# Window values projected straight into token-major form, instead of transposed after the projection

## The reference

```python
h = rmsnorm(x, norm_mix[l])
aq, ak, av, bq, bk, bv, cin = split_last(h @ w_in[l], IN_SIZES)      # widths 256,128,128,512,512,512,1024
o_win = window_gqa(aq, ak, av, ...)      # 4 query heads, 2 key/value heads of 64, keys within +-128 tokens
o_diff = diff_attention(bq, bk, bv, ...) # 4 heads, two softmax maps each, all 1024 keys
o_rwkv = rwkv7_bidir(cin, ...)           # centred short convolution, two delta-rule scans
x = x + jnp.concatenate([o_win, o_diff, o_rwkv], axis=-1) @ w_out[l]
x = x + cross_attn(rmsnorm(x, norm_cross[l]), mem_n, ...)
gate, up = jnp.split(rmsnorm(x, norm_ffn[l]) @ ffn_w_gu[l], 2, axis=-1)
x = x + (jax.nn.silu(gate) * up) @ ffn_w_down[l]
return rmsnorm(x, norm_final)
```

## Time and profile before

| | |
|---|---|
| Time, median of 3 runs | 1676.02 us (1674.48 to 1683.61) |
| The profiled execution's own time | 1674.48 us |
| Its span in the trace | 1672.7 us |
| PE busy | 1605.2 us (96%) |
| PE weight loads busy | 1324.3 us (79%) |
| DVE, ACT, POOL busy | 805.0, 734.5, 759.3 us |
| Share of PE in the chain that ended last | 87% |

### The profile page before, as it was taken

The page is one execution under the profiler, slowest core; times in us unless marked ns, Lnnn a source line. Parts: engine busy times, 40 slices in busy tenths (PEclk is TensorE's granted clock), DMA queues, the critical chain, the costliest instruction groups (busy, mean ns, idle before and its releaser), DMA issues.

```text
span 1672.7 us, 31783 instructions
## 1 busy us (share of the span) xinstructions
PE 1605.2 (96%) x13137; PEld 1324.3 (79%) x13137; DVE 805.0 (48%) x1290; ACT 734.5 (44%) x1389; POOL 759.3 (45%) x670
## 2 busy tenths in 40 slices
PE   7999999999977999989999999999999999999998
PEld 6888878777855778868888878788888888888886
DVE  4104888427364765553432657543343344244336
ACT  5324888643365544333454754223223323322325
POOL 3222665122164733364455015546547556555651
PEclk9999999999979999999999999999999999999999
DMA  6110000121000010017233002112012102111203
GB/s 209 51 50 25 1 1 1 70 70 44 20 0 7 4 54 5 4 64 252 95 106 103 19 14 94 39 51 76 26 51 76 50 27 76 63 38 51 75 2 126
DMA packets 62541, 91.61 MB, mean 55 GB/s; under 512 B 4434, under 2 KB 45552, under 8 KB 62144
## 3 DMA queue, kind: packets, MB, share of 16 engines
q1 hardware_dynamic: 61456, 87.08, 15.5%
q0 software_dynamic: 944, 2.52, 0.6%
HBM read 83.29 MB, written 6.29 MB: 54 GB/s over the span
## 4 chain that ended last, share of the span: by engine, by line
PE 87%; DVE 6%; ACT 3%; issue 2%; POOL 2%; DMA 1%; SPq 0%; DVEq 0%; ACTq 0%; POOLq 0%
PE PS L2696 7%; PE PS L2698 7%; PE PS L2697 7%; PE PS L2329 7%; PE PS L2047 5%; PE PS L2050 5%; PE PS L2048 5%; PE PS L2703 5%; PE PS L2704 5%; PE PS L2705 5%; PE PS L2060 4%; PE PS L2062 4%; PE PS L2061 4%; PE PS L2144 3%; PE PS L2188 3%; PE PS L2401 2%
## 5 line engine op out<-in xcount | busy, mean ns | idle before, releaser
L608 POOL TENSOR_TENSOR WL<-RAW,WH 128x512 fp32r<-128x512 f32 x120 | 170.8, 1434 | 354.1 <-ACT WH L877 353.4
L2047 PE MATMUL PS<-HH,WH 128*128 128x512 f32 x416 | 164.3, 395 | 0.3 <-DVE SM L1465 0.3
L1992 DVE TENSOR_TENSOR X<-PS,X 128x512 f32<-128x512 f32 x160 | 110.6, 692 | 109.1 <-PE PS L2705 109.1
L784 POOL TENSOR_TENSOR WL<-WU_RAW,WH 128x512 fp32r<-128x512 f32 x60 | 77.3, 1296 | 188.6 <-ACT WH L861 188.6
L2048 PE MATMUL PS<-HL,WH 128*128 128x512 f32 x416 | 161.9, 389 | 0.0
L877 ACT ACTIVATE WH<-RAW 128x512 fp32r<-128x512 f32 x121 | 74.3, 630 | 149.5 <-PE PS L2050 54.1
L2703 PE MATMUL PS<-WH,FH 128*128 128x512 f32 x352 | 137.0, 389 | 1.7 <-DVE FL L1946 1.7
L2704 PE MATMUL PS<-WL,FH 128*128 128x512 f32 x352 | 136.9, 389 | 0.0
L2705 PE MATMUL PS<-WH,FL 128*128 128x512 f32 x352 | 136.9, 389 | 0.0
L2050 PE MATMUL PS<-HH,WL 128*128 128x512 f32 x416 | 133.5, 389 | 0.0
L2698 PE MATMUL PS<-HH,WL 128*128 128x512 f32 x320 | 124.5, 389 | 0.0
(11 more groups left out here) (404 smaller groups left out, 3879.9 us busy)
## 6 DMA issues: line engine op xcount, KB each, us to landing
WD_RAW<-in_ffn_w_down SPq DMA_DIRECT2D x44, 256.0 KB, 2.6
RAW<-in_w_in SPq DMA_DIRECT2D x43, 256.0 KB, 2.8
WG_RAW<-in_ffn_w_gu SPq DMA_DIRECT2D x20, 512.0 KB, 4.2
WU_RAW<-in_ffn_w_gu SPq DMA_DIRECT2D x20, 512.0 KB, 4.5
RAW<-in_w_out SPq DMA_DIRECT2D x32, 256.0 KB, 2.7
XT<-in_x SPq DMA_DIRECT2D x8, 512.0 KB, 6.6
X<-in_x SPq DMA_DIRECT2D x8, 512.0 KB, 6.2
RAW<-in_x_wq SPq DMA_DIRECT2D x16, 256.0 KB, 2.7
```

What stands on the lines that cost most here:

```text
L608: pool.tensor_tensor(w_low, raw_at(p), w_high.bitcast(F32), ALU.subtract).then_inc(w_lo, 2 if p < N_VAL else 1)
L784: pool.tensor_tensor(w_low, quarter(kind, i, name), w_high.bitcast(F32), ALU.subtract).then_inc(w_lo, 1)
L2047: pe.matmul(where(ct, i), wh[:, k, c], ah(kt)[:, t0:t0 + n], start=first and starts(ct, i), stop=False, skip_group_check=True)
```

## The change

The projection of job 9 gets a form of its own. The key columns stay feature-major: `feature_job` with `cts=(0,)`, six matmuls of 512 columns per k-tile, into banks 4 and 5. The value columns are projected token-major through the hook `extra`, which was there but unused in this place: per k-tile, eight token tiles by three `token_mm` matmuls, whose stationary operand is a 128 x 128 block of `HH` or `HL` and whose moving operand is the 128 value columns of `WH` or `WL`. They go to banks 6 and 7. The sum over k is accumulated in PSUM over all four pieces, as before. ACT then copies banks 6 and 7 straight to `AV`. The eight transposes in job 10, the second copy, and the wait of PE before job 11 go away.

```diff
@@ -960,7 +960,8 @@
                         a.then_inc(job_evac, 1)
                     else:
                         act.wait_ge(r_kk, 2)
-                        act.activation(TMP[:, 512 * (i - 2):512 * (i - 2) + 512], bank[i], ACT.Copy).then_inc(job_evac, 1)
+                        act.activation(AV[:, 4 * (i - 2):4 * (i - 2) + 4, :], bank[i].rearrange("p (t c) -> p t c", t=4),
+                                       ACT.Copy).then_inc(job_evac, 1)
 
             def k_first_parts(h):
                 if h == 1:
@@ -1063,11 +1064,6 @@
 
             for j in range(6, NJ):
                 hi(min(4 * j + 10, 4 * NJ))
-                if j == J_AK + 1:
-                    act.wait_ge(v_mm, NT)
-                    for b in range(2):
-                        a = act.activation(AV[:, 4 * b:4 * b + 4, :], PS[:, 6 + b, :].rearrange("p (t c) -> p t c", t=4), ACT.Copy)
-                    a.then_inc(v_lo, 1)
                 evac_proj(j)
                 if j == 6:
                     act.wait_ge(r_conv, 1)
@@ -2125,7 +2121,17 @@
                     pe.wait_ge(vec_c, 1)
                 pe.wait_ge(job_evac, 4 * (j - 1))
                 c0, bank = proj_cols[j], 4 * (j % 2)
-                feature_job(4, hh, hl, lambda ct, i: PS[:, bank + 2 * ct + i, :], after=after)
+                if c0 == AK0:
+
+                    def values(wh, wl, k, kt, first, last):
+                        for tt in range(NT):
+                            mm = token_mm(PS[:, bank + 2 + tt // 4, P * (tt % 4):P * (tt % 4) + P], wh[:, k, P:2 * P], wl[:, k, P:2 * P], hh, hl, kt, tt,
+                                          first and tt % 4 == 0, last)
+                        return mm
+
+                    feature_job(4, hh, hl, lambda ct, i: PS[:, bank + i, :], cts=(0,), extra=values)
+                else:
+                    feature_job(4, hh, hl, lambda ct, i: PS[:, bank + 2 * ct + i, :], after=after)
 
             def d_scores(u, maps=(0, 1)):
                 h, qb = u // 8, u % 8
@@ -2259,14 +2265,7 @@
                 if q == 2:
                     w_scores(2)
 
-            def window_values(q):
-                if q == 1:
-                    pe.wait_ge(job_evac, 4 * (J_AK + 1))
-                    for tt in range(NT):
-                        mm = pe.transpose(PS[:, 6 + tt // 4, P * (tt % 4):P * (tt % 4) + P], TMP[:, tt * P:(tt + 1) * P], ID)
-                    mm.then_inc(v_mm, 1)
-
-            within = {6: last_head, 7: low_rank, 8: key_norms, 10: window_values, 11: first_windows}
+            within = {6: last_head, 7: low_rank, 8: key_norms, 11: first_windows}
             for j in range(6, NJ):
                 if j == 7:
                     pe.wait_ge(hm_evac, 8)
@@ -2276,8 +2275,6 @@
                     pe.wait_ge(r_std, 2)
                 if j >= 10:
                     pe.wait_ge(qw_lo, j - 9)
-                if j == 11:
-                    pe.wait_ge(v_lo, N_VAL // 2 + 1)
                 proj(j, within.get(j))
             pe.wait_ge(job_evac, 4 * NJ)
```

## The result

| | before | after |
|---|---|---|
| Median of 20 runs each, us | 1677.44 (1673.0 to 1688.74) | 1688.13 (1683.59 to 1692.76) |
| Ratio after / before, 95% interval | | 1.006 (1.0047 to 1.0074) |
| Profiled execution, us | 1674.48 | 1693.37 |
| Its span, us, and mean granted clock | 1672.7, 0.991 | 1691.3, 0.986 |

The change makes the kernel slower: by the ratio and its interval 10 us (8 to 12). The profiled execution of the changed kernel is 18.9 us above that of before, more than the medians say, and the first thing to settle is which part of that belongs to the change.

A forecast was written before the change was run, and what follows sets the result against it. The prediction took PE to bound the kernel: +11.8 us for job 9's narrow matmuls and -0.9 us for the transposes gave +10.9 us on 1674.48 us, 1685.4 us, stated as a median of 1686.0 us, range 1682 to 1708 us.

The forecast's parts named there:

- Slower by more than 0.5%: Whole kernel: the measured time would be slower by more than 0.5%, 8.4 us; chance 0.86.
- What bounds the kernel: Stretch from 390 to 452 us: PE bounds it without idle time; a microsecond of PE is one of the kernel.
- The price of a narrow matmul: Job 9's value half: 192 matmuls at 0.118 us, 22.7 us, replacing 10.9 us of wide ones, +11.8 us.
- The lower bound of 0.0667 us: Job 9: price of one narrow matmul if only its 128 moving columns counted, 12.8 us in all.
- The transposes: Job 10: the eight transposes go, on PE and on the path, -0.9 us.
- ACT, waits, DMAs at nothing: Around jobs 9 to 11: the dropped ACT copies, dropped PE waits and unchanged DMA pieces are worth nothing.
- The granted clock in job 9: Job 9: PE's granted clock stays at 2.4 GHz, as before the change.
- What follows behind: Behind job 11: its 2.15 us wait moves along and absorbs nothing; the whole +10.9 us passes to the end.
- Plain float32 pace: Job 9: each narrow fp32r matmul takes two passes, 0.232 us, 44.6 us in all; +32.8 us, 1707.3 us; chance 0.12.
- The load does not bind: Job 9: narrow matmuls take 0.0667 us as loads do not limit; +1.0 us, 1675.5 us; chance 0.06.
- The +3.8 us: Jobs 9 and 10: at 81 ns per narrow matmul the sum is 15.6 - 10.9 - 0.9, no change that can be told.
- Part of the delay absorbed: Later stages: a transfer or DVE chain not hanging on job 9 hides perhaps half; +5 us, 1680 us; chance 0.06.

The follow-up runs named there:

- the kernel with fewer loads: Changed kernel with WH and WL value columns joined as one 256-column moving operand for HH, 128 loads instead of 192: job 9 25.82 us, ratio 1.0041 to the kernel before.
- the two halvings: Changed kernel, narrow matmuls cut to 64 moving columns (job 9 87.74 us, ratio 1.0423), or to 64 stationary columns (job 9 2.0 us longer than in the changed kernel).

## Why the prediction was right, point by point

**The total.** Forecast 1686.0 us in a range of 1682 to 1708, of which 1682 to 1690 were the forecast's own; measured 1688.13. Of the 2.1 us between them, 1.4 are that the 20 runs of the kernel before have a median of 1677.44 and not the 1676.02 from which the forecast started. The sum was 1.0 us too high on PE, so that the medians also lie 10.7 us apart is partly luck. "Slower by more than 0.5%" is met by the ratio of 1.006, but its interval reaches down to 1.0047.

**What bounds the kernel.** Right. PE has no idle time in jobs 9 and 10 of either kernel, and the chain stays on PE. The start of the next stage moved by 9.81 us, which is what the two jobs together changed (10.69 - 0.83 = 9.86).

**The price of a narrow matmul: the term that was mis-sized.** The text took "0.118 us, between the nearest by width and the nearest by type: 22.7 us". It measured 0.1123 us with its switches and 21.57 us in all, 1.1 us less. The bound "0.110 us each" from the transposes was the closest of the rows, and the steady pace of 0.1115 us is 1.5 ns above it. The choice between rows went by the number format and by the width. What decides is neither: up to 128 moving columns it is the number of stationary ones. Plain float32 at 128 columns (0.116) and fp32r at 256 columns (0.120) lie a little higher, and no run shows why. The 256 columns alone are 0.107 us at 0.417 ns each, close to the load, and in the kernel with fewer loads they cost nothing beyond it. The lower bound of 0.0667 us was no bound: 0.060 us were measured with 128 moving columns, with half the stationary ones. Job 9 was to last 33 to 34 us and lasted 32.45, which is the same 1.1 us. The reason given, that "halving the columns of the stream in rows 6 should leave the load as the limit", is shown by the two halvings.

The Trainium skill, "TensorE: Matmul & The Clock Gate", section "LDWEIGHTS (loading the stationary operand)", gave 107 ns a load by its rule of columns over 1.2 GHz, and with it an estimate of +9.6 us for this part. The part measured 21.57 - 10.88 = +10.7 us. The steady pace is 4.5 ns above the rule and 6.5 ns below the 0.118 taken, so the rule was the better estimate of the pace. In the sum the two lie equally far off, 1.1 us on either side. The half-stationary kernel agrees with the direction of that rule and not with its size: 0.060 us a matmul where it would give 53 ns for 64 columns, and there the moving columns may be what counts.

**The transposes.** Predicted -0.9 us. Measured -0.83 in the changed kernel, -0.89 alone, +0.89 when put back. Right.

**ACT, waits, DMAs at nothing.** Right. ACT's second copy went and its next copy waited 10.20 us for PE instead of 9.81. No new wait of PE shows in the three jobs. Of "ACT and DVE with longer waits for PE", ACT's waits and DVE's for the keys are longer.

**The granted clock in job 9.** Predicted as before, and it was 1.00. The 64-column experiment suggests that this was less safe than the text made it. The same loads at the same pace with half as many columns behind them lost the clock after 4.4 us of narrow matmuls. The forecast didn't price that case.

**What follows behind.** Job 11 and the 2.15 us wait behind it moved and absorbed nothing. The sum by PE is +9.86 us, the prediction was +10.9.

**The rivals.** Plain float32 pace: out, one row for each and 0.1115 us apart. The load does not bind: out, by the pace and by the halved moving columns. The +3.8 us by the Trainium skill, "TensorE: Matmul & The Clock Gate", section "Back-to-back issue gap" (81 ns) did not come either: no stream here with 128 stationary columns in each load was that fast. Part of the delay absorbed: out up to the next stage, where 9.81 of 9.86 us arrive. Behind it the medians show 10 us (8 to 12), so half of it was not hidden later.

## What to carry to other kernels

In an fp32r projection whose matmuls have 128 moving columns or fewer, count stationary blocks, not columns. With a new block of 128 columns for each matmul the price was 0.111 us at 64 and at 128 moving columns, 0.120 at 256 and 0.2267 at 512, so the same arithmetic in 128-column matmuls cost twice what it cost in 512-column ones. Eight PE transposes of the result at 0.89 us were far cheaper than a projection that comes out transposed at +10.7 us: keep the long dimension moving, and turn the small result afterwards. And before you put a difference of two profiles down to a change, compare stretch by stretch up to where the change ends, profile the kernel before twice, and put the granted clock beside each time: here 8.8 us of 18.6 arose behind the change, no more than two profiles of the kernel before differ there.

## What was not expected of the hardware

- The granted clock fell from the level of 2.4 to that of 1.2 GHz in a stream without any idle time of PE: 64-column matmuls with a load each, after 4.4 us of narrow matmuls, and it came back and fell again within the job. The pace went from 0.111 to 0.2133 us, and a load beside it showed 0.33 us instead of 0.19. Why it fell is not shown. This is one kernel, profiled once; both of its executions show it in the time (1749.0 and 1753.14 us). The stream of 128 columns at the same pace kept 1.00 in every profile of the changed kernel, and so did the 384 matmuls with half the stationary columns.
- A load of 64 stationary columns costs at most 0.060 us, where 128 cost 0.111, so a half-full block does not pay for a full one.
- One and the same kernel differed by 12.1 us in span between two profiles, 10.7 of it in a single stage at a clock of 0.91 against 0.96. On one chip, 23 runs of it lay between 1674.23 and 1688.23 us at mean clocks of 0.991 to 0.985. Intervals of 0.3% from 5 rounds did not always hold what PE's stretches gave; at equal clock the gap was 1.0 to 1.6 us.
